# A two-layer decoder trunk in split fp32: attention as one unrolled stream of steps, with low parts placed in the zero halves of the head operands

## The reference: what is computed

```python
def memory_attention(qm, mk, mv):
    s = jnp.einsum('bshd,bmhd->bhsm', qm, mk).astype(jnp.float32) * (HEAD_DIM ** -0.5)
    p = jax.nn.softmax(s, axis=-1).astype(mv.dtype)
    return jnp.einsum('bhsm,bmhd->bshd', p, mv)

def reference(...):
    for i in range(DEPTH):
        mk, mv = jnp.split(mem @ w_mem_kv[i], 2, axis=-1)
        if i % 2 == 0:
            h = x @ a_w_in[j]
            q, k, v, qm = jnp.split(h, [DIL_WIDTH, 2 * DIL_WIDTH, 3 * DIL_WIDTH], axis=-1)
            mix = dilated_attention(q, k, v)      # three patterns, merged by their sums
        else:
            h = x @ b_w_in[j]
            u, v, qm = jnp.split(h, [SGU_WIDTH, 2 * SGU_WIDTH], axis=-1)
            mix = causal_chunk_sgu(jax.nn.gelu(u), jax.nn.gelu(v), ...)
        mo = memory_attention(qm, mk, mv)
        y = jnp.concatenate([mix, mo], axis=-1) @ w_out[i]
        x = layer_norm(DN_ALPHA * x + y, ...)
        f = (jax.nn.silu(x @ w_gate[i]) * (x @ w_up[i])) @ w_down[i]
        x = layer_norm(DN_ALPHA * x + f, ...)
```

## Time and profile before

| what | value |
|---|---|
| runs | 2519.93 to 2521.85 us, median 2521.57 |
| span of the profiled execution | 2518.2 us; no time of its own is listed for it |
| TensorE matmul busy | 2393.0 us, 95% |
| VectorE busy | 1058.1 us, 42% |
| ScalarE busy | 519.3 us, 21% |
| POOL busy | 1056.4 us, 42% |
| DMA | 127.41 MB, mean 51 GB/s |

### The profile page before, as it was taken

How to read it: one execution, slowest core, us unless ns; L and a number is a source line. 1 busy time by engine, 2 the same in 40 slices (tenths; PEclk the granted TensorE clock), 3 DMA queues, 4 the chain that set the end, 5 groups by cost and what they waited for, 6 DMA issues and landing times.

```text
span 2518.2 us, 31661 instructions
## 1 busy us (share of the span) xinstructions
PE 2393.0 (95%) x12120; PEld 2031.8 (81%) x12120; DVE 1058.1 (42%) x2027; ACT 519.3 (21%) x1069; POOL 1056.4 (42%) x498
## 2 busy tenths in 40 slices
PE   7999999999889999999999898999899999999997
PEld 6888888888678888888887788877688888888885
DVE  5455444466742222222225735556822222222226
ACT  4344433331300000000003532212200000000002
POOL 4311122263754444444443775423854333344443
PEclk9999999999999999999999999999999999999998
DMA  4111001131021111111111021211021111111111
GB/s 152 43 43 42 25 16 42 59 109 59 17 67 50 50 50 50 50 50 50 45 47 42 26 72 47 68 34 34 17 77 49 42 50 50 50 50 50 50 34 67
DMA packets 160453, 127.41 MB, mean 51 GB/s; under 512 B 11520, under 2 KB 146304, under 8 KB 160384
## 3 DMA queue, kind: packets, MB, share of 16 engines
q1 hardware_dynamic: 147808, 114.31, 14.8%
q10 hardware_dynamic: 12576, 12.16, 1.6%
HBM read 122.26 MB, written 4.19 MB: 50 GB/s over the span
## 4 chain that ended last, share of the span: by engine, by line
PE 78%; DVE 10%; issue 7%; ACT 3%; POOL 1%; DMA 0%; DVEq 0%; ACTq 0%; POOLq 0%
PE ps L254 26%; PE ps L255 25%; PE ps L256 25%; DVE XTl L758 2%; PE ps L402 1%; DVE XR L845 1%; DVE st L782 1%; DVE XR L693 1%; ACT mP L497 1%; DVE PTl L582 1%; ACT PTh L506 1%; DVE V L1112 1%; PE ps L651 0%; ACT dP L497 0%; DVE VSl L1129 0%
## 5 line engine op out<-in xcount | busy, mean ns | idle before, releaser
L243 POOL TENSOR_TENSOR Wh<-raw,zcol 128x1024 fp32r<-128x1024 f32 x190 | 366.0, 1926 | 1246.2 <-PE ps L256 968.5
L254 PE MATMUL ps<-XTh,Wh 128*128 128x512 f32 x1760 | 691.3, 393 | 15.2 <-DVE hid L959 9.2
L255 PE MATMUL ps<-XTl,Wh 128*128 128x512 f32 x1760 | 688.3, 391 | 0.0
L256 PE MATMUL ps<-XTh,Wl 128*128 128x512 f32 x1760 | 687.9, 391 | 0.0
L246 POOL TENSOR_TENSOR Wl<-raw,Wh 128x1024 fp32r<-128x1024 f32 x190 | 474.2, 2496 | 14.9
L254 PEld LDWEIGHTS ps<-XTh,Wh 128*128 128x128 f32 x1760 | 332.6, 189 | 84.3 <-DVE XTl L758 15.7
L256 PEld LDWEIGHTS ps<-XTh,Wl 128*128 128x128 f32 x1760 | 332.5, 189 | 69.8
L255 PEld LDWEIGHTS ps<-XTl,Wh 128*128 128x128 f32 x1760 | 332.8, 189 | 67.8
L693 DVE TENSOR_TENSOR XR<-XR,ps 128x512 f32<-128x512 f32 x416 | 281.5, 685 | 228.6 <-PE ps L256 228.6
L959 DVE TENSOR_TENSOR hid<-silu,ps 128x512 f32<-128x512 f32 x88 | 60.4, 686 | 691.5 <-PE ps L256 691.5
L254 PE MATMUL ps<-Wh,hidh 128*128 128x512 f32 x704 | 277.3, 394 | 24.1 <-DVE XR L691 15.4
(11 more groups left out here) (164 smaller groups left out, 2855.8 us busy)
## 6 DMA issues: line engine op xcount, KB each, us to landing
raw<-in_w_gate SPq DMA_DIRECT2D x44, 512.0 KB, 3.8
raw<-in_w_up SPq DMA_DIRECT2D x44, 512.0 KB, 3.8
raw<-in_w_down SPq DMA_DIRECT2D x44, 512.0 KB, 3.7
raw<-in_a_w_in SPq DMA_DIRECT2D x20, 512.0 KB, 5.1
raw<-in_w_out SPq DMA_DIRECT2D x16, 512.0 KB, 3.8
raw<-in_b_w_in SPq DMA_DIRECT2D x14, 512.0 KB, 3.8
dB<-in_c_bias SPq DMA_DIRECT2D x12, 512.0 KB, 3.7
raw<-in_w_mem_kv SPq DMA_DIRECT2D x8, 512.0 KB, 3.8
```

The source lines that it names most:

```text
L243: nc.gpsimd.tensor_tensor(Wh[:, slot, :], raw[:, turn, :], zcol[:, 0:1].to_broadcast([P, UNIT]), ALU.add).then_inc(high_done, 1)
L254: nc.tensor.matmul(dst, wh, xh, start=first, stop=False)
L255: nc.tensor.matmul(dst, wh, xl, start=False, stop=False)
L256: return nc.tensor.matmul(dst, wl, xh, start=False, stop=last)
```

## The change

Attention of a layer is one stream of steps, written out without a loop, one step per item of all pairs in order (`attention_pe`, `attention_act`, `attention_dve`). In step j TensorE issues the even score tile of the item to come, the two transposes of item j, half of this step's projection, the odd score tile, the product of item j - 1 with the values, the other half of the projection, and the transposes of the reciprocals of a chunk that closed two items ago. `plan` deals the projections out: the second halves of a pair's queries, keys and values in its steps 0 to 2, the turning of the values at 3, the first halves for the next pair in steps 5 to 10, the turning at 11. All but four first ones go through one PSUM bank (`PROJ`), and a projection waits until the one before is out of it (`proj_free_pe`). Scores have the other three banks of the lower half, in units of up to 512 columns; tiles of more than 512 columns are two units, and the second unit's logits take the first's maximum as their start.

The halves that were zero now hold low parts. A head's high queries stand in both halves, and its keys have the high part in one half and the low part in the other; two products (high queries, low queries with the other half still zero) replace three. The values have low columns beside the high ones; two products replace three, and give two half sums on different partitions, which ScalarE copies (`o_copy_act`) and VectorE adds (`halves_dve`). Each head has its own half of the bank. The zero block of the probabilities is one fixed block that products address. The reciprocal is taken directly in its wide form. The last pair's mixed output lies in a free part of `XTl`, and the bias of a pair is loaded later in SyncE's order.

The core of the diff:

```diff
-    PTh = at("PTh", [P, 2, 4, 2, P], F32R, A_WH + 12 * KB)
-    Kh = at("Kh", [P, S], F32R, A_WH + 20 * KB)
-    PTl = at("PTl", [P, 2, 4, 2, P], F32R, A_WL + 12 * KB)
-    Kl = at("Kl", [P, S], F32R, A_WL + 20 * KB)
+    PTh = at("PTh", [P, 17, P], F32R, A_WH + 12 * KB)
+    PTl = at("PTl", [P, 17, P], F32R, A_WL + 12 * KB)
+    Ob = at("Ob", [P, 2 * P], F32, A_WH + 22 * KB + 512)
+    Os = at("Os", [P, 2 * P], F32, A_WL + 22 * KB + 512)
+    RB = [at(f"RB{i}", [P, P], F32, w + 23 * KB + 512) for i, w in enumerate((A_WH, A_WL))]
+    mixL = at("mixL", [P, S], F32, A_XTL + 7 * 4 * KB)
...
-            if free:
-                pe.wait_ge(*g("logits", pi * 16 + free))
-            nb = max(256, w) if w <= 512 else w // 2
-            for i in range(1 if w <= 512 else 2):
-                dst = bank(banks[i], nb)
-                ks = slice(i * nb, (i + 1) * nb)
-                q0 = slice(qt * P, (qt + 1) * P)
-                mm = three(dst, bf.Qh[:, hd, q0], bf.Ql[:, hd, q0], Kh[:, ks], Kl[:, ks], True, True)
-            mm.then_inc(g("scores"), 1)
...
-            if hd == 1 and last:
-                pe.wait_ge(*g("rden_wide", pi * 4 + c + 1))
-                for q in range(2):
-                    mm = nc.tensor.transpose(bank(6 + c % 2, P, 256 + q * P),
-                                             bf.RB[:, q, :, :].rearrange("p a d -> p (a d)"), ident[:, :])
-                mm.then_inc(g("rden_turned"), 1)
...
+    PROJ = 3
...
+    def plan(g, i):
+        kind = kind_of(g)
+        after = g + 1 if g not in (7, 9) else None
+        steps = []
+        if kind == "mem":
+            if i < 2:
+                steps.append(("q", g, 1, 4 * i, 4 * i + 4))
+            elif after is not None and 4 <= i < 7:
+                steps.append(("qkv"[i - 4], after, 0, 0, KT))
+            elif after is not None and i == 7:
+                steps.append(("turn", after, 0, 0, 0))
+        elif i < 3:
+            steps.append(("qkv"[i], g, 1, 0, KT))
+        elif i == 3:
+            steps.append(("turn", g, 1, 0, 0))
+        elif after is not None and 5 <= i < 11:
+            k = 4 * ((i - 5) % 2)
+            steps.append(("qkv"[(i - 5) // 2], after, 0, k, k + 4))
+        elif after is not None and i == 11:
+            steps.append(("turn", after, 0, 0, 0))
+        return steps
...
+    def proj_free_pe(pe, what, g, h):
+        if what == "k":
+            pe.wait_ge(*at_("q_low", 2 * (rank(g, "q", h) + 1)))
+        elif what == "v":
+            pe.wait_ge(*at_("k_low", 2 * (rank(g, "k", h) + 1)))
+        elif rank(g, "v", 0) >= 1:
+            pe.wait_ge(*at_("v_low", KV[g] + h))
+            pe.wait_ge(*at_("q_low", 2 * rank(g, "q", h)))
...
+    def split_steps(steps):
+        first, second = [], []
+        for what, g, h, k0, k1 in steps:
+            m = (k0 + k1 + 1) // 2
+            if what == "turn":
+                second.append((what, g, h, k0, k1))
+            else:
+                first.append((what, g, h, k0, m))
+                second.append((what, g, h, m, k1))
+        return first, second
...
+        for h in range(n_units(kind, n)):
+            u = unit(g, n, h)
+            if u >= 3:
+                pe.wait_ge(*at_("logits", u - 2))
+            nb = max(256, unit_cols(g, n, h))
+            K = bf.K(g, hd, h)[:, 0:nb]
+            nc.tensor.matmul(bank(u % 3, nb), bf.Qh[:, hd, qt * P:(qt + 1) * P], K, start=True, stop=False)
+            nc.tensor.matmul(bank(u % 3, nb), bf.Ql[:, hd, qt * P:(qt + 1) * P], K, start=False,
+                             stop=True).then_inc(at_("scores"), 1)
...
+        dst = bank(6 + C % 2, 2 * P, 256 * hd)
+        for k in range(nk):
+            V = bf.Vs[:, v_slot(g, lo + k), hd, :]
+            none = kind == "dil" and last and k == nk - 1
+            nc.tensor.matmul(dst, V, pt_blocks(PTh, gi, k, none), start=first and k == 0, stop=False)
+            mm = nc.tensor.matmul(dst, V, pt_blocks(PTl, gi, k, none), start=False, stop=last and k == nk - 1)
...
+    def attention_pe(pe, L, ready=lambda g, i: None):
+        seq = stream(L)
+        scores_pe(pe, seq[0][0], 0)
+        scores_pe(pe, seq[0][0], 1)
+        for j in range(len(seq) + 2):
+            if j < len(seq):
+                g, i = seq[j]
+                s, lo, nk, first, last = items(kind_of(g))[i]
+                ready(g, i)
+                ng, ns = (g, s + 1) if s < 7 else (g + 1, 0)
+                ahead = first and ng in STREAMS[L]
+                one, two = split_steps(plan(g, i))
+                if ahead:
+                    scores_pe(pe, ng, 2 * ns)
+                turn_probs_pe(pe, g, i, 0)
+                turn_probs_pe(pe, g, i, 1)
+                fill_pe(pe, one)
+                if ahead:
+                    scores_pe(pe, ng, 2 * ns + 1)
+            if 1 <= j <= len(seq):
+                pv_pe(pe, *seq[j - 1])
+            if j < len(seq):
+                fill_pe(pe, two)
+            if closing(L, j - 2):
+                recip_pe(pe, *closing(L, j - 2))
...
+    def q_act(act, g, h):
+        bf = buf(g)
+        cs = slice(h * 512, h * 512 + 512)
+        b = bank(proj_bank(g, "q", h))
+        act.wait_ge(*at_("q_proj", rank(g, "q", h) + 1))
+        for hd in range(2):
+            nc.scalar.activation(bf.Qh[own(hd), hd, cs], b[own(hd), :], ACT.Copy, scale=QSCALE).then_inc(at_("q_high"), 1)
+        for hd in range(2):
+            act.wait_ge(*at_("q_high", 2 * rank(g, "q", h) + hd + 1))
+            nc.scalar.activation(bf.Qh[other(hd), hd, cs], bf.Qh[own(hd), hd, cs].bitcast(F32),
+                                 ACT.Copy).then_inc(at_("q_again"), 1)
...
+    def o_copy_act(act, g, c):
+        C = 4 * g + c
+        act.wait_ge(*at_("pv", ITEMS[g] + item_of(kind_of(g), 2 * c + 1) + 1))
+        for hd in range(2):
+            nc.scalar.activation(Ob[own(hd), :], bank(6 + C % 2, 256, 256 * hd)[other(hd), :],
+                                 ACT.Copy).then_inc(at_("o_copied"), 1)
...
-            nc.vector.reciprocal(rden[:, t0:t0 + 4], den[:, t0:t0 + 4]).then_inc(g("rden"), 1)
-            dve.wait_ge(*g("rden", pi * 4 + c + 1))
-            src = rden[:, t0:t0 + 4].rearrange("p (h i) -> p i h", h=2).unsqueeze(3).to_broadcast([P, 2, 2, HD])
-            nc.vector.tensor_copy(bf.RB[:, :, :, :], src).then_inc(g("rden_wide"), 1)
...
-        for i, (s, lo, nk, first, last) in enumerate(its):
-            if first and s < 7:
-                logits(2 * s + 2)
-            if last and not first and s < 7:
-                logits(2 * s + 3)
-            if last and kind == "dil":
-                zero(i)
-            pt_low(i, 0)
-            if first and last and s < 7:
-                logits(2 * s + 3)
-            pt_low(i, 1)
-            if last and s % 2 == 0 and s >= 2:
-                mix(s // 2 - 1)
-            if last and s % 2 == 1:
-                rden_of(s // 2)
...
+    def k_dve(dve, g, h):
+        n = proj_cols(g, "k")
+        for hd in range(2):
+            K = buf(g).K(g, hd, h)
+            dve.wait_ge(*at_("k_high", 2 * rank(g, "k", h) + hd + 1))
+            nc.vector.tensor_tensor(K[other(hd), 0:n], bank(proj_bank(g, "k", h), n)[own(hd), :],
+                                    K[own(hd), 0:n].bitcast(F32), ALU.subtract).then_inc(at_("k_low"), 1)
...
+        G = 16 * g + n
+        if G >= 3 and not (g == 8 and n < 3):
+            g3, n3 = (G - 3) // 16, (G - 3) % 16
+            dve.wait_ge(*at_("turned", 2 * (ITEMS[g3] + item_of(kind_of(g3), n3 // 2)) + n3 % 2 + 1))
...
+        for h in range(n_units(kind, n)):
+            w = unit_cols(g, n, h)
+            u = unit(g, n, h)
+            dve.wait_ge(*at_("scores", u + 1))
+            b0 = S - P - qt * P + 512 * h
+            bias = bf.zero[:, :] if kind == "mem" else B[:, hd, b0:b0 + w]
+            nc.vector.memset(tick[:, 16 * h + n:16 * h + n + 1], 0.0)
+            if h:
+                dve.wait_ge(*at_("logits", u))
+            nc.vector.tensor_tensor_reduce(bf.Pb[:, G % 3, 512 * h:512 * h + w], bank(u % 3, w), bias, -1.0,
+                                           mneg[:, n:n + 1] if h else 3e38, ALU.add, ALU.min,
+                                           mneg[:, n:n + 1]).then_inc(at_("logits"), 1)
...
+    def rden_dve(dve, g, c):
+        C = 4 * g + c
+        dve.wait_ge(*at_("probs", 16 * g + 4 * c + 4))
+        if C >= 1:
+            dve.wait_ge(*at_("rden_turned", C))
+        for q in range(2):
+            src = den[:, 4 * c + q:4 * c + q + 3:2].unsqueeze(2).to_broadcast([P, 2, HD])
+            ins = nc.vector.reciprocal(RB[q][:, :].rearrange("p (a d) -> p a d", a=2), src)
+        ins.then_inc(at_("rden"), 1)
+    def halves_dve(dve, g, c):
+        C = 4 * g + c
+        dve.wait_ge(*at_("o_copied", 2 * (C + 1)))
+        if C >= 1:
+            dve.wait_ge(*at_("mixed", C))
+        for hd in range(2):
+            ins = nc.vector.tensor_tensor(Os[own(hd), :], bank(6 + C % 2, 256, 256 * hd)[own(hd), :], Ob[own(hd), :],
```

(21 more changed lines are left out.)

737 lines of the change are left out of this document (340 added, 397 removed).

## The result

| | before | after |
|---|---|---|
| time, us, median (lowest to highest) of 4 runs | 2521.7 (2519.9 to 2522.2) | 2613.7 (2612.6 to 2615.0) |
| ratio, 95% interval | | 1.0364 (1.035 to 1.0379) |
| span of the profiled execution, us | 2518.2 | 2612.5 |
| granted clock, mean over the span | 0.984 | 0.958 |

The change makes the kernel 92 us slower. The forecast was 2565, 43 us slower, so the sign was right and the size less than half.

The account below looks back on a forecast made before the run. TensorE's own work was taken as the bound. Memory pairs -8.6, five dilated periods +32.5, last pair +12.3 and layer 1 +7.1 made +43, 2518.2 to 2561; with the median 3.4 above the span, 2565 us, range 2505 to 2645.

Parts of the forecast that it names:

- The work that leaves TensorE: All attention pairs: one of three score and value products goes, 8.8 us a dilated pair, 68 us in all.
- Waits of the walk: Middle dilated pair followed through twelve steps: TensorE waits 18 us instead of 2.3, period 79.7 us instead of 73.2.
- (a): Steps 5, 7, 9, 11: second transpose waits for odd logits and low part, 2.0 to 2.3 us, 1.2 at 11.
- (b): One PSUM bank for all projections: hand-overs lose 1.5 and 1.0 us at steps 1 and 2, 1.1 to 1.2 at 0.
- (c): Steps 7 and 9: late odd logits and the projection bank's hand-over together, TensorE loses 4.5 and 6.1 us.
- step 4: Dilated pair: TensorE loses 1.3 us on a score bank, as logits 10 stands behind the mixing.
- clock falls in the new gaps: Rival, chance 0.08: after the 4.5 and 6.1 us gaps products run at 1.2 GHz, +30 us, 2595 in all.
- -8.6: Memory pairs of layer 0: first dilated step forecast at 118.1 us where it was 126.7.
- +7.1: Layer 1: scores start at 1417.2 us, memory pairs end at 1490.6 us against 1483.5.
- TensorE stays the bound: Rival, chance 0.17: dilated pair's waits fall below 11 us; about 2508 us with half the waits, 2454 with none.
- no net change: Rival, chance 0.08: waits and saved TensorE work cancel, 2519 to 2525 us.
- the dear reciprocal: Rival, chance 0.22: a 128-column reciprocal takes 2 us or more, VectorE bound in memory steps too; 2600 to 2641 us.

Follow-up runs that it names:

- the run at a clock of 1.00: Changed kernel plus products nobody reads in all six large gaps of a dilated pair; 2590.5 us.
- Two mends worth 11.3 and 19.4 us: Each against the changed kernel: low parts ahead of the odd logits, 2602.4 us; projections whole at steps 5, 7 and 9, 2594.3 us. Both together: 2562.4 us.

## Why the prediction was right in sign and short in size

- **The work that leaves TensorE**: held. 62 us a period agrees with 68.5 busy at a clock of 0.91, and within 1.4 us with the run at a clock of 1.00. The warning case, TensorE busy over 95%, is far off at 80%. (The four stretches of before add up to 571.9 us, not 572.3; nothing hangs on it.)
- **Waits of the walk**, (a), (b), (c) and step 4: some 18 us forecast, 17.0 measured, at the steps named. Single ones were off: steps 7 and 9 show 2.25 and 2.84 us of hand-over behind 2.2 of stall, 4.4 and 5.0 together where my totals were 4.5 and 6.1. I had missed that memory pairs' ninth score waits for ScalarE's second copy of the queries (2 x 1.1). The walk treated (a) and (c) as things one could mend apart; the run with the low parts first shows that at steps 7 and 9 they are one chain.
- **The step that failed is the rival "clock falls in the new gaps", which I gave 0.08 and left out of the sum.** Its two gaps of 4.5 and 6.1 us were in the walk, with the 5.5 us gap of the earlier trace rows as the model for each. "Against it: at step 7 a transpose lies in the gap" was the wrong argument: behind two gaps of 2.2 us with two transposes between them the clock read 0.54. Its price was 2 x 2.7 us a pair; it came at three places, step 5 too, some 1.5 us each. The five periods are 29 of the 49 us missing. With the gaps filled 4.4 of the 5.8 us a period came back, so at least 22 of the 29 are this term; the other 1.4 a period stay open.
- **The same term in the memory pairs**: "-8.6" was -0.4 and "+7.1" was +15.2. I put 2 us there for a slow clock at the head of layer 1 only, and counted 7.6 us of saved work in each. The third product put back shows that work worth 0.4 and 0.9 us, and some 5.5 and 4.8 us of it lost to the clock; gaps filled with products nobody reads were not tried in these pairs.
- **A term put at nothing**: the walk of layer 1 starts from 1413.1 us, the last low part of its input, as if only the attention of layer 0 could move it. It came at 1493.8, 80.7 later, where layer 0's attention accounts for 76.8. The two traces run 76.8 us apart up to 1476.8. Behind that TensorE has two projections of the memory tokens, 48 products of 256 columns, among the transposes of the input, where before it had one, 24 products, behind all of them. That this order costs the 3.9 us was not tested. With them, 15.2 is 3.9 and 11.3 behind the input, for 7.1 forecast.
- **The last pair**: +12.3 forecast, +15.6 measured, clock 0.92; the 3.3 us between were not taken apart.
- **TensorE stays the bound, no net change**: rightly small. **The range** held the result by luck: its upper end, 2645, stood there for the dear reciprocal, and a reciprocal takes 0.92 us, not 2 or more.

## What to carry to other kernels

Where a forecast makes TensorE wait in several places a few microseconds apart, price the work behind each gap at the lower clock, and put that into the sum and not among the rivals. Before taking products away, ask whether they were what kept the clock up: in the memory pairs putting 7.6 us of products back cost 0.4 and 0.9 us. And to learn what a clock costs, fill the gaps with products nobody reads; it needs no change of order.

When several operands go through one bank, the hand-over ends when the longest chain of the engines that empty it does, and mending one wait can uncover the next: count a mend only with the others done. A better order did not save the change either: the best of the other orders tried here is still 28.6 us behind the kernel before.

## What the runs showed that I had not expected

- Two gaps of 2.2 us with two transposes between them are followed by products at 1.2 GHz, and so are gaps of 1.09 and 1.93 us with a few products between them (clock 0.51). The Trainium skill ("TensorE: Matmul & The Clock Gate", Part 1) says "the default state is throttled, and activity releases the throttle"; the gaps filled with products agree, clock 0.91 to 1.00.
- More work made the kernel faster: 80 products more -12.6 us, 220 more -23.2 us.
- Two mends worth 11.3 and 19.4 us gave 51.3 together, 20.6 more than their sum; in the traces more of the surplus is waits than clock.
